# A fused three-layer block on one Trainium2 core: the state space layer's gate, skip and norm move from tokens by features to features by tokens, and the norm's root scales the output block

## The chip, the core and the metric

One core of a Trainium2 chip runs the whole program. The metric is the device time of one execution in microseconds, from the first to the last instruction with the start and the end around them; lower is better. The engines are TensorE (PE, matmuls, with its weight loads PEld), VectorE (DVE), ScalarE (ACT), GpSimd (POOL) and SyncE (SP), which here only issues transfers.

## The reference

The block takes x of 256 tokens by 2048 features through three layers: a Mamba2 state space layer, a sliding window attention layer, and a neighbourhood attention layer with an MLP. Only the first is touched. Its essence:

```python
z, xbc, dt = split(x @ w_in)                 # z: 4096 columns, 8 groups of 512
xs, B, C   = split(silu(conv4(xbc)))         # 64 heads of 64, 8 groups
y = ssd_chunked(xs, dt, a, B, C) + xs * d_skip[head]
y = y * silu(z)
yg = y.reshape(tokens, 8, 512)
yg = yg * rsqrt(mean(yg**2, over the 512) + 1e-5)
h = (yg.reshape(tokens, 4096) * norm_w) @ w_out
x = layernorm(ALPHA * x + h)
```

In ssd_chunked the part that a head adds to its outputs carries, per head and token, a factor exp(cumulated dt*a) (called the row factor below).

## The kernel before

**Products.** Every weight tile is 128 x 2048 fp32 and is split into a high part (whi, written by ACT) and a low part (wlo, written by DVE), and a product is the sum of three: high by high, low by high, high by low. The program is a list of units, one weight tile each. A unit of form "A" gives 128 features by 256 tokens: 16 matmuls of 512 columns (L1066, both parts of the activations side by side) and 16 of 256 columns with the low weights (L1070). A unit of form "B" gives 256 tokens by 512 features of a partial product, in two blocks t of 12 matmuls of 512 columns (L1087, L1089, L1091). An A unit reads its low weights only in its second half, a B unit in its third matmul.

**Rings.** whi, wlo and the raw tiles have three places each. The split of unit u+2 is written while unit u runs and may begin when unit u-1 has left the place; the transfer of unit u+5 is issued by SP when the split of u+2 has read its place. The order of the work on every engine is one hand-written script: in unit u each engine does, in this order, the emptying of unit u-1 (`late`), the split of u+2 (`hi` on ACT, `lo` on DVE), what is left of u-1 (`post`), the unit itself on PE, and the steps that a timetable puts after it. All engines run their own queue in order and meet at semaphores.

**The state space layer.** For each of the 8 groups g there are 14 units: B, C, four x units (A form; their emptying has a convolution over tokens on DVE, L1893 to L1769), four z units (B form, tokens by features, emptied by ACT's silu into zs), and the four output units ao of the group before (B form, summed into the residual XR on DVE, L1951). Four z units of group 0 stand first. Beside them runs a state space computation per group in numbered steps n = 0..13 (0..15 in groups 0 and 1, where most steps are 2 later, `late = 2`). In the units of group g the step n of group g follows unit start+n. Step by step: dif_heads (ACT L1499, L1501) writes decays for 8 heads; px turns x to tokens by features (PE L1152); xd multiplies by dt (DVE L2036) and xdk by the skip (L2045); e0, e1 are exponentials (ACT L1525), m0, m1 masks (DVE L2053); heads_out (PE L1181, L1183) gives o0 and o1, features by tokens; ACT copies them out (yT, L1529), PE turns them to tokens by features (turn_out, L1194, 8 transposes), DVE applies row factor, skip, gate and the sum of squares (L2061 to L2070), POOL takes the root (L2495), DVE scales by it (yt, L2076), PE turns y back (8 transposes, L1167), and ACT and DVE write its high part A2h (L1519) and low part A2l (L1769), which the ao units read.

**Places in PSUM.** Banks 0 to 3 go round among the units; banks 4 to 7 ("side" 0 to 3) hold the small products. A use of a side bank waits until the use before it has been emptied; the table EMPTIES names the step that empties each use.

In the notes below u17 to u20 are the units z(1,0) to z(1,3) of group 1, and u21 is ao(0,0), the first output unit.

## Time and profile before

| | |
|---|---|
| median of three runs | 2109.36 us (2108.74 to 2109.99) |
| the profiled execution: its time | 2108.5 us |
| its span, first to last instruction | 2106.5 us |
| granted TensorE clock | 1.000 |
| PE busy | 2099.5 us, 100% of the span |
| DVE busy | 1545.3 us, 73% |
| ACT busy | 1113.8 us, 53% |
| POOL busy | 52.3 us, 2% |
| DMA | 407.01 MB, mean 193 GB/s |

The state space layer's units take about the first 690 us. A matmul's record lasts longer than the time to the next one, since they overlap in the array: what a matmul costs is read from start to start. Busy shares of DVE and ACT are means over three layers; what counts is whether a split or a side product is ready when PE comes to it.

### The profile page before, as it was taken

Reading aid. Unit: us, or ns where it says so; the run is one execution under the profiler, and the core shown is the slowest. Engines: PE = TensorE matmul, PEld = TensorE weight load, DVE = VectorE, ACT = ScalarE, POOL = GpSimd, SP = SyncE. Lnnn points to the kernel's source line nnn. Section 1 sums busy time; section 2 is a strip of 40 time slices with the busy share of each in tenths; the row PEclk is TensorE's granted clock in tenths of the full one; section 3 lists DMA queues with packets and bytes.
Section 4 is the critical chain, followed back from the end, with each engine's and each line's share of the span. In section 5 each row is a group of like instructions: output and inputs, shape, how many; then the busy total and the mean of one; then the engine's idle time right before and its main releaser. Section 6 shows DMA issues by size and latency. Waiting matters only on the chain.

```text
span 2106.5 us, 27150 instructions
## 1 busy us (share of the span) xinstructions
PE 2099.5 (100%) x10752; PEld 1765.4 (84%) x10752; DVE 1545.3 (73%) x2068; ACT 1113.8 (53%) x1366; POOL 52.3 (2%) x42
## 2 busy tenths in 40 slices
PE   9999999999999999999999999999999999999999
PEld 7888888888888888888888888888888888888887
DVE  7888878768778877675675556556778688787775
ACT  6765565564554556563555445545545455455452
POOL 0000000000000000000010011000000000000000
PEclk9999999999999999999999999999999999999999
DMA  8555555555554644345564544455575666566663
GB/s 314 200 213 188 187 194 180 199 194 180 187 183 177 211 170 164 140 153 196 180 225 172 196 177 166 167 181 204 194 240 188 219 212 201 222 187 212 240 178 141
DMA packets 63710, 407.01 MB, mean 193 GB/s; under 512 B 7200, under 2 KB 9952, under 8 KB 16224
## 3 DMA queue, kind: packets, MB, share of 16 engines
q1 hardware_dynamic: 61568, 390.60, 51.5%
q0 software_dynamic: 2016, 14.68, 3.9%
q8 instruction: 85, 1.39, 0.3%
q14 instruction: 41, 0.34, 0.0%
HBM read 403.09 MB, written 2.16 MB: 192 GB/s over the span
## 4 chain that ended last, share of the span: by engine, by line
PE 99%; DVE 1%; DMA 0%; SPq 0%; POOL 0%; issue 0%; ACT 0%; DVEq 0%
PE bank L1066 22%; PE bank L1087 18%; PE bank L1091 17%; PE bank L1089 17%; PE bank L1070 11%; PE bank L1105 2%; PE bank L1103 2%; PE bank L1107 2%; PE bank L1181 1%; PE bank L1329 1%; PE bank L1265 1%; PE bank L1287 0%; PE bank L1224 0%; PE bank L1317 0%; PE bank L1194 0%; DMA raw<-wst 0%
## 5 line engine op out<-in xcount | busy, mean ns | idle before, releaser
L1809 DVE TENSOR_TENSOR wlo<-raw,whi 128x2048 fp32r<-128x2048 f32 x318 | 727.5, 2288 | 258.9 <-ACT whi L1393 226.5
L1393 ACT ACTIVATE whi<-raw 128x2048 fp32r<-128x2048 f32 x318 | 608.3, 1913 | 289.3 <-PE bank L1091 274.8
L1066 PE MATMUL bank<-A,whi 128*128 128x512 f32 x2000 | 479.2, 392 | 0.0
L1066 PEld LDWEIGHTS bank<-A,whi 128*128 128x128 f32 x2000 | 369.0, 188 | 74.3 <-issue 1.2
L1087 PE MATMUL bank<-whi,A 128*128 128x512 f32 x832 | 330.7, 397 | 0.7 <-ACT whi L1383 0.7
L1091 PE MATMUL bank<-wlo,A 128*128 128x512 f32 x832 | 325.1, 391 | 0.1
L1089 PE MATMUL bank<-whi,A 128*128 128x512 f32 x832 | 324.4, 390 | 0.0
L1087 PE MATMUL bank<-whi,A2h 128*128 128x512 f32 x800 | 314.1, 393 | 0.0
L1091 PE MATMUL bank<-wlo,A2h 128*128 128x512 f32 x800 | 311.6, 390 | 0.0
L1089 PE MATMUL bank<-whi,A2l 128*128 128x512 f32 x800 | 311.5, 389 | 0.0
L1070 PEld LDWEIGHTS bank<-A,wlo 128*128 128x128 f32 x2000 | 256.4, 191 | 9.7
L1070 PE MATMUL bank<-A,wlo 128*128 128x256 f32 x2000 | 259.4, 283 | 0.0
L1091 PEld LDWEIGHTS bank<-wlo,A 128*128 128x128 f32 x832 | 156.2, 188 | 35.7 <-DVE wlo L1797 3.1
L1087 PEld LDWEIGHTS bank<-whi,A 128*128 128x128 f32 x832 | 156.3, 188 | 34.4 <-issue 2.7
L1089 PEld LDWEIGHTS bank<-whi,A 128*128 128x128 f32 x832 | 156.4, 188 | 31.1 <-DVE A L2201 0.7
L1091 PEld LDWEIGHTS bank<-wlo,A2h 128*128 128x128 f32 x800 | 150.2, 188 | 31.6
L1087 PEld LDWEIGHTS bank<-whi,A2h 128*128 128x128 f32 x800 | 150.2, 188 | 30.6 <-issue 0.3
L1089 PEld LDWEIGHTS bank<-whi,A2l 128*128 128x128 f32 x800 | 150.3, 188 | 30.4
L1809 DVE TENSOR_TENSOR wlo<-W,whi 128x2048 fp32r<-128x2048 f32 x56 | 128.2, 2290 | 45.0 <-ACT whi L1393 44.1
L1393 ACT ACTIVATE whi<-W 128x2048 fp32r<-128x2048 f32 x56 | 107.4, 1921 | 69.3 <-DVE W L1820 46.3
L1428 ACT ACTIVATE W<-bank 128x256 f32<-128x256 f32 x60 | 23.0, 384 | 179.9 <-PE bank L1070 179.9
L2495 POOL TENSOR_TENSOR SM<-SM 128x2 f32<-128x2 f32 (+2 forms) x24 | 39.7, 1657 | 1393.5 <-DVE SM L2070 644.9
(259 smaller groups left out, 1874.7 us busy)
## 6 DMA issues: line engine op xcount, KB each, us to landing
raw<-wst SPq DMA_DIRECT2D x313, 1024.0 KB, 4.8
W<-wst SPq DMA_DIRECT2D x33, 1024.0 KB, 5.0
W<-wst POOLq DMA_DIRECT2D x9, 1024.0 KB, 8.2
W<-cum_scratch SPq DMA_DIRECT2D x8, 1024.0 KB, 7.0
W<-rows SPq DMA_DIRECT2D x21, 256.0 KB, 5.6
raw<-wst POOLq DMA_DIRECT2D x5, 1024.0 KB, 8.1
raw<-wst SPq DMA_DIRECT2D x16, 256.0 KB, 7.4
W<-nabias SPq DMA_DIRECT2D x16, 160.0 KB, 4.1
```

Of the source, the lines that this page charges most:

```text
L1066: e.matmul(o[:, :], whi[:, s, k * P:(k + 1) * P], A1[:, k, :, :].rearrange("p h t -> p (h t)"), start=k == 0, stop=False)
L1070: last = e.matmul(o[:, T:2 * T], wlo[:, s, k * P:(k + 1) * P], A1h[:, k, :], start=False, stop=k == KT - 1)
L1087: e.matmul(o, h, wh, start=opens and k == 0, stop=False)
L1089: e.matmul(o, low, wh, start=False, stop=False)
L1091: last = e.matmul(o, h, wl, start=False, stop=t in shut(tag) and k == 3)
L1103: e.matmul(o, h, wh, start=name in ("a", "b", "d", "f") and k == 0, stop=False)
L1105: e.matmul(o, low, wh, start=False, stop=False)
L1107: last = e.matmul(o, h, wl, start=False, stop=k == 3)
L1393: e.activation(whi[:, u % 3, :], raw_of(u), ACT.Copy).then_inc(*hi.inc((u, 3)))
L1428: e.activation(W[:, M_R + i % 4 * T:M_R + (i % 4 + 1) * T], rest, ACT.Copy).then_inc(*rest_a.inc(u))
L1809: e.tensor_tensor(wlo[:, u % 3, :], raw_of(u), whi[:, u % 3, :], ALU.subtract).then_inc(*lo.inc((u, 3)))
L2495: return e.tensor_tensor(SM[:, to:to + n], SM[:, src:src + n], SM[:, S_MH:S_MH + n], ALU.pow)
```

## The change

The gate, the skip, the row factor and the sum of squares now work on features by tokens, the layout in which heads_out writes.

- z of groups 1 to 7 is computed by A units (`zf`, features by tokens): 28 B units become A units. ACT copies the second half of each out, DVE adds the first, and after the fourth ACT does one silu over 1024 columns. z of group 0 stays as it was, is copied out plain, and 8 new transposes on PE (step 1) turn it; ACT's silu follows them.
- The row factor comes from DRAM: it is stored once to exp_scratch, and for every group SP loads two halves of 64 partitions (exp_load, step 8, 9 in group 1), 256 KB each as they land.
- ACT forms skip times x (`k0` to `k3`, step 8). DVE multiplies o0 and o1 by the row factor (y1), adds the skip (y2), multiplies by the gate (y3), each of the last two in one instruction of 1024 columns. ACT squares y3 (`sq`) and writes A2h from it directly, DVE writes A2l from it. The yT copies, turn_out, the back transposes, xdk and yt are gone.
- The sum of squares over 512 features: two additions on DVE (a0, a1), then two matmuls of one column on PE (`rs`, step 12 + late) into side bank 3, a small DVE step (ms, step 13 + late) and POOL's root. The root multiplies the output block as it is emptied from PSUM (`mul_add(x, ps, r, x)` in the ao units). So the A2 tiles hold y without the root.
- The residual's factor ALPHA is applied ahead, by two ACT instructions over 2048 columns in group 0, step 4.
- The transposes of the row factor (2 of the 6 in L1133) are gone.

The diff, cut to its core:

```diff
-            u += b(("z", g), "a_w_in", g * 512)
+            u += [("A", ("zf", g, i), "a_w_in", g * 512 + i * P) for i in range(4)]
...
-        if g == 0:
-            run(("ssd", 0), start, 12)
-            mid[at["z", 1, 0]].append(("ssd", 0, 12))
-            run(("ssd", 0), at["z", 1, 0], 16, 13)
-        elif g == 1:
-            run(("ssd", 1), start, 16)
-        elif g < NG - 1:
-            run(("ssd", g), start, 14)
-        else:
-            run(("ssd", g), start, 10)
-            mid[start + 10].append(("ssd", g, 10))
-            run(("ssd", g), start + 10, 14, 11)
+        run(("ssd", g), start, 16 if g < 2 else 14)
...
-            "dts": lambda: dt_v("copy"), "cb": lambda g: ssd_v("kcb", g), "px": lambda g, t: ssd_v(f"xdk{t}", g),
-            "o": lambda g, hh: ssd_a(f"yT{hh}", g), "to": lambda g, t: ssd_v(f"y1_{t}", g),
-            "yq": lambda g, pr: ssd_v(f"tl{2 * pr + 1}", g),
+            "dts": lambda: dt_v("copy"), "cb": lambda g: ssd_v("kcb", g), "px": lambda g, t: ssd_v(f"xd{t}", g),
+            "o": lambda g, hh: ssd_v(f"y1_{hh}", g), "rs": lambda g: ssd_v("ms", g), "zq": lambda i: ssd_a(f"zs{i}", 0),
...
+                if n == 12 + late:
+                    yield ("rs", g), 3
...
+            def exp_load(g):
+
+
+                w.wait_ge(s_exst, 16)
+                if g:
+                    w.wait_ge(*ssd_p("rs", g - 1))
+                src = ex_scratch.rearrange("(g f i) t -> g i f t", f=4, i=2)
+                for i in range(2):
+                    to = W[64 * i:64 * (i + 1), W_EX:W_EX + 1024].rearrange("p (f t) -> p f t", f=4)
+                    e.dma_start(to, src[g, i:i + 1].partition_broadcast(64)).then_inc(s_ex, 16)
+
             def ssd(g, n):
                 late = 2 if g < 2 else 0
+                if n == (9 if g == 1 else 8):
+                    exp_load(g)
...
+                if g == 0 and n == 1:
+                    w.wait_ge(s_ko, 16)
+                    for i in range(2):
+                        o = free(("zq", i))
+                        for t in range(NT):
+                            w.wait_ge(*evac_a((at["z", 0, 3], t)))
+                            for f in range(2):
+                                tr = e.transpose(o[:, f * T + t * P:f * T + (t + 1) * P],
+                                                 z0[t][:, (2 * i + f) * P:(2 * i + f + 1) * P], ident)
+                        tr.then_inc(*ssd_p.inc(f"z{i}", 0))
...
+                if n == 12 + late:
+                    o = free(("rs", g))
+                    w.wait_ge(*ssd_v("a1", g))
+                    for t in range(NT):
+                        mean = e.matmul(o[:, t:t + 1], ex[:, t * P:(t + 1) * P], tri[:, P:P + 1], start=True, stop=True)
+                    mean.then_inc(*ssd_p.inc("rs", g))
...
+                elif kind == "zf":
+                    w.wait_ge(*ssd_v("y3", tag[1] - 1))
+                    e.activation(zs[:, tag[2], :], rest, ACT.Copy).then_inc(*rest_a.inc(u))
...
+                elif tag[0] == "zf" and tag[2] == 3:
+                    w.wait_ge(*evac_v((u, 0)))
+                    e.activation(zs, zs, ACT.Silu).then_inc(*zs_a.inc("s", tag[1]))
...
+                if g == 0 and n == 4:
+                    for t in range(NT):
+                        w.wait_ge(s_xr[t], 16)
+                        e.activation(XR[:, t, :], XR[:, t, :], ACT.Identity, scale=ALPHA).then_inc(*xr_a.inc(str(t)))
+                if n in (7 + late // 2, 8 + late // 2):
+                    decays(g, n - 7 - late // 2)
+                if n == 8:
+                    w.wait_ge(s_co, 16)
+                    if g:
+                        w.wait_ge(*ssd_a("th3", g - 1))
+                        w.wait_ge(*ssd_v("tl3", g - 1))
+                    else:
+                        w.wait_ge(*ssd_p("z1", 0))
+                    for f in range(4):
+                        c = C_DSK + 4 * g + f
+                        w.wait_ge(*conv_a("silu", 6 * g + 2 + f))
+                        e.activation(yf[:, f, :], xf[2 + f], ACT.Identity,
+                                     scale=CO[:, c:c + 1]).then_inc(*ssd_a.inc(f"k{f}", g))
+                if n == 10 + late:
+                    w.wait_ge(*ssd_v("y3", g))
+                    e.activation(ex, y, ACT.Square).then_inc(*ssd_a.inc("sq", g))
+                    if g >= 2:
+                        w.wait_ge(*mm((at["ao", g - 2, ND - 1], 1)))
+                    for f in range(4):
+                        e.activation(A2h[:, 4 * (g % 2) + f, :], yf[:, f, :], ACT.Identity,
+                                     scale=norm_w(g, f)).then_inc(*ssd_a.inc(f"th{f}", g))
...
-                    x = xr(t, tag[2])
-                    if j == 0:
-                        w.wait_ge(*residual_ready(t, tag[2], "ao"))
-                        mul_add(x, x, ALPHA, ps, ALU.mult, ALU.add).then_inc(*evac_v.inc((u, t)))
-                    else:
-                        w.wait_ge(*evac_v((at["ao", j - 1, tag[2]], t)))
-                        e.tensor_tensor(x, ps, x, ALU.add).then_inc(*evac_v.inc((u, t)))
+                    x, r = xr(t, tag[2]), S_T + 4 + j % 2 * 2 + t
+                    w.wait_ge(*(evac_v((at["ao", j - 1, tag[2]], t)) if j else residual_ready(t, tag[2], "ao")))
+                    w.wait_ge(*ssd_g("r", j))
+                    mul_add(x, ps, SM[:, r:r + 1], x, ALU.mult, ALU.add).then_inc(*evac_v.inc((u, t)))
...
+                if n in (9 + late, 10 + late):
+                    hh = n - 9 - late
+                    half = ex[:, hh * 512:(hh + 1) * 512]
+                    w.wait_ge(*ssd_p(f"o{hh}", g))
+                    w.wait_ge(s_ex, 32 * (g + 1))
+                    e.tensor_tensor(half, side[SIDE["o", g, hh][0]][:, :], half, ALU.mult).then_inc(*ssd_v.inc(f"y1_{hh}", g))
+                if n == 10 + late:
+                    w.wait_ge(*ssd_v("y1_1", g))
+                    w.wait_ge(*ssd_a("k3", g))
+                    e.tensor_tensor(y, ex, y, ALU.add).then_inc(*ssd_v.inc("y2", g))
+                    w.wait_ge(*ssd_v("y2", g))
+                    w.wait_ge(*(zs_a("s", g) if g else ssd_a("zs1", 0)))
+                    e.tensor_tensor(yf, yf, zs, ALU.mult).then_inc(*ssd_v.inc("y3", g))
                 if n == 11 + late:
-                    w.wait_ge(*ssd_p("to", g))
-                    if g:
-                        w.wait_ge(*ssd_p("q1", g - 1))
-                    for t in range(NT):
-                        c = W_DTS + 128 + 64 * t + g * HG
-                        e.tensor_tensor(by_head(y[t]), by_head(side[SIDE["to", g, t][0]][:, :]),
-                                        per_head(W[:, c:c + HG]), ALU.mult).then_inc(*ssd_v.inc(f"y1_{t}", g))
-                        w.wait_ge(*ssd_v(f"y1_{t}", g))
-                        e.tensor_tensor(y[t], y[t], W[:, W_XD + t * 512:W_XD + (t + 1) * 512],
-                                        ALU.add).then_inc(*ssd_v.inc(f"y2_{t}", g))
-                        w.wait_ge(*ssd_v(f"y2_{t}", g))
-                        w.wait_ge(*evac_a((at["z", g, 3], t)))
-                        e.tensor_tensor(y[t], y[t], zs[:, t, :], ALU.mult).then_inc(*ssd_v.inc(f"y3_{t}", g))
-                        w.wait_ge(*ssd_v(f"y3_{t}", g))
-                        e.tensor_tensor_reduce(out=zs[:, t, :], in0=y[t], in1=y[t], scale=1.0 / 512, scalar=EPS,
-                                               op0=ALU.mult, op1=ALU.add,
-                                               accum_out=SM[:, S_T + 4 + t:S_T + 5 + t]).then_inc(*ssd_v.inc(f"ss{t}", g))
-                if n == 12 + late:
-                    w.wait_ge(*ssd_g("r", g))
-                    for t in range(NT):
-                        e.tensor_scalar(y[t], y[t], SM[:, S_T + 6 + t:S_T + 7 + t], None,
-                                        ALU.mult).then_inc(*ssd_v.inc(f"yt{t}", g))
+                    w.wait_ge(*ssd_a("sq", g))
+                    e.tensor_tensor(ex[:, 0:512], ex[:, 0:512], ex[:, 512:1024], ALU.add).then_inc(*ssd_v.inc("a0", g))
+                    w.wait_ge(*ssd_v("a0", g))
+                    e.tensor_tensor(ex[:, 0:T], ex[:, 0:T], ex[:, T:2 * T], ALU.add).then_inc(*ssd_v.inc("a1", g))
+                    if g >= 2:
+                        w.wait_ge(*mm((at["ao", g - 2, ND - 1], 1)))
+                    for f in range(4):
+                        kt = 4 * (g % 2) + f
+                        w.wait_ge(*ssd_a(f"th{f}", g))
+                        mul_add(A2l[:, kt, :], yf[:, f, :], norm_w(g, f), A2h[:, kt, :], ALU.mult,
+                                ALU.subtract).then_inc(*ssd_v.inc(f"tl{f}", g))
                 if n == 13 + late:
-                    for pr in range(2):
-                        ps = side[SIDE["yq", g, pr][0]]
-                        w.wait_ge(*ssd_p(f"q{pr}", g))
-                        if g >= 2:
-                            w.wait_ge(*mm((at["ao", g - 2, ND - 1], 1)))
-                        w.wait_ge(*ssd_a(f"th{2 * pr + 1}", g))
-                        for i in range(2):
-                            f = 2 * pr + i
-                            kt = 4 * (g % 2) + f
-                            mul_add(A2l[:, kt, :], ps[:, i * T:(i + 1) * T], norm_w(g, f), A2h[:, kt, :],
-                                    ALU.mult, ALU.subtract).then_inc(*ssd_v.inc(f"tl{f}", g))
+                    w.wait_ge(*ssd_p("rs", g))
+                    e.tensor_scalar(SM[:, S_T + 2:S_T + 4], side[SIDE["rs", g][0]][:, 0:2], 1.0 / 512, EPS, ALU.mult,
+                                    ALU.add).then_inc(*ssd_v.inc("ms", g))
...
-                if n == 11 + (2 if g < 2 else 0):
-                    w.wait_ge(*ssd_v("ss1", g))
-                    rsqrt(S_T + 6, S_T + 4, 2).then_inc(*ssd_g.inc("r", g))
+                if n == 13 + (2 if g < 2 else 0):
+                    w.wait_ge(*ssd_v("ms", g))
+                    if g >= 2:
+                        w.wait_ge(*evac_v((at["ao", g - 2, ND - 1], 1)))
+                    rsqrt(S_T + 4 + g % 2 * 2, S_T + 2, 2).then_inc(*ssd_g.inc("r", g))
```

How this moves instructions, at the places that the prediction speaks of.

ACT, around u17 and u18 in group 0's steps 12: before, from the silu of the last x unit of group 1 to the split of u20 (whi is written by L1393; L1499 and L1501 are the decays of group 1's first three heads):

```order
L1442 ACTIVATE W<-W 128x256 [waits conv_v]
L1499 ACTIVATE W<-W 128x256 [waits ssd_p0,cum_in]
L1501 ACTIVATE W<-W 128x128
L1499 ACTIVATE W<-W 128x256
L1501 ACTIVATE W<-W 128x128
L1499 ACTIVATE W<-W 128x256
L1501 ACTIVATE W<-W 128x128
L1393 ACTIVATE whi<-raw 128x2048 [waits mm_done,raw_in2]
```

Now (whi is written by L1399, the decays are L1512 and L1514, L1542 is sq, L1546 writes A2h, L1437 copies the second half of zf out):

```order
L1453 ACTIVATE W<-W 128x256 [waits conv_v]
L1542 ACTIVATE W<-W 128x1024 [waits ssd_v0]
L1546 ACTIVATE A2h<-W,CO 128x256 x4
L1512 ACTIVATE W<-W 128x256 [waits ssd_p0,cum_in]
L1514 ACTIVATE W<-W 128x128
L1512 ACTIVATE W<-W 128x256
L1514 ACTIVATE W<-W 128x128
L1512 ACTIVATE W<-W 128x256
L1514 ACTIVATE W<-W 128x128
L1437 ACTIVATE W<-bank 128x256 [waits mm_done]
L1399 ACTIVATE whi<-raw 128x2048 [waits raw_in2]
```

sq, which waits for DVE's y3, and the four A2h writes now stand ahead of the decays and of the split of u20.

DVE, the same units: before, from cb's copy of group 1 (L2027) through the splits of u20 and u21 (L1809), with the scaling by the root (L2076) and xd of group 1 (L2036) between:

```order
L2027 TENSOR_TENSOR W<-bank,KO 128x384 [waits ssd_p1]
L1809 TENSOR_TENSOR wlo<-raw,whi 128x2048 [waits mm_done,hi_done,raw_in2]
L2076 TENSOR_SCALAR W<-W,SM 128x512 [waits ssd_rms]
L2076 TENSOR_SCALAR W<-W,SM 128x512
L2036 TENSOR_TENSOR W<-bank,W 128x512 [waits ssd_p1]
L2036 TENSOR_TENSOR W<-bank,W 128x512
L1809 TENSOR_TENSOR wlo<-raw,whi 128x2048 [waits mm_done,hi_done,raw_in0]
```

Now, from the split of u19 (L1831): y1 of o1 (L2073), y2, y3, cb's copy (L2049), the emptying of the first zf unit (L1899), the split of u20, then a0, a1, A2l and xd of group 1 (L2058):

```order
L1831 TENSOR_TENSOR wlo<-raw,whi 128x2048 [waits hi_done,raw_in1]
L2073 TENSOR_TENSOR W<-bank,W 128x512 [waits ssd_p0]
L2077 TENSOR_TENSOR W<-W 128x1024 [waits ssd_v0]
L2080 TENSOR_TENSOR W<-W 128x1024 [waits ssd_v0]
L2049 TENSOR_TENSOR W<-bank,KO 128x384 [waits ssd_p1]
L1899 TENSOR_TENSOR W<-bank,W 128x256 [waits second_half_out,mm_done]
L1831 TENSOR_TENSOR wlo<-raw,whi 128x2048 [waits hi_done,raw_in2]
L2083 TENSOR_TENSOR W<-W 128x512 [waits ssd_a0]
L2085 TENSOR_TENSOR W<-W 128x256 [waits ssd_v0]
L1791 SCALAR_TENSOR_TENSOR A2l<-W,CO,A2h 128x256 [waits ssd_a0] x4
L2058 TENSOR_TENSOR W<-bank,W 128x512 [waits ssd_p1]
L2058 TENSOR_TENSOR W<-bank,W 128x512
```

a0, a1, A2l and xd of group 1 all stand behind the split of u20 in DVE's queue.

PE: the end of px of group 1 (L1176), the unit u19 (zf(1,2)), the new rs pair of group 0 (L1184, waits for both ssd_v semaphores) and the start of u20. Before, this place had no product of group 0; the back transposes (L1167) stood inside u19:

```order
L1176 MATMUL bank<-KO,W 128x128 [waits conv_a] x3
L1176 MATMUL bank<-KO,W 128x128 x4
L1080 MATMUL bank<-A,whi 128x512 [waits hi_done,emptied_v]
L1080 MATMUL bank<-A,whi 128x512 x15
L1084 MATMUL bank<-A,wlo 128x256 [waits lo_done]
L1084 MATMUL bank<-A,wlo 128x256 x15
L1184 MATMUL bank<-KO,W 128x1 [waits ssd_v0,ssd_v1]
L1184 MATMUL bank<-KO,W 128x1
L1080 MATMUL bank<-A,whi 128x512 [waits hi_done,emptied_v]
```

rs writes side bank 3, whose last use before it is px of group 1 (second block), emptied by xd of group 1 on DVE; hence the wait on two semaphores, one for a1 of group 0 and one for xd of group 1. PE does not begin u20 before rs has gone.

## Rows read from the trace of the kernel before

**Rows 1.** The page: the span, and the chain that ended last by engine.
```profile
span 2106.5 us, 27150 instructions
...
PE 99%; DVE 1%; DMA 0%; SPq 0%; POOL 0%; issue 0%; ACT 0%; DVEq 0%
```

**Rows 2.** Timeline of PE, group 6's x units: start us, duration us, then the instruction.
```profile
500.65 3.82 PE L1066 MATMUL bank<-A,whi 128*128 128x512 f32 x16
...
506.22 3.82 PE L1066 MATMUL bank<-A,whi 128*128 128x512 f32 x16
```

**Rows 3.** Timeline of PE, group 2's ao units and the transposes beside them.
```profile
304.20 0.66 PE L1194 MATMUL bank<-KO,W 128*128 128x128 f32 x4
304.61 0.48 PE L1087 MATMUL bank<-whi,A2h 128*128 128x512 f32 x1
304.93 0.39 PE L1089 MATMUL bank<-whi,A2l 128*128 128x512 f32 x1
...
309.94 0.40 PE L1091 MATMUL bank<-wlo,A2h 128*128 128x512 f32 x1
...
310.53 0.48 PE L1087 MATMUL bank<-whi,A2h 128*128 128x512 f32 x1
...
316.11 0.39 PE L1087 MATMUL bank<-whi,A2h 128*128 128x512 f32 x1
...
321.55 0.39 PE L1087 MATMUL bank<-whi,A2h 128*128 128x512 f32 x1
...
326.76 0.40 PE L1091 MATMUL bank<-wlo,A2h 128*128 128x512 f32 x1
...
327.79 2.53 PE L1066 MATMUL bank<-A,whi 128*128 128x512 f32 x10
```

**Rows 4.** Timeline of ACT in group 0; in brackets the idle time before, and its releaser.
```profile
35.36 1.28 ACT L1483 ACT_TABLE_LOAD   x1
...
67.53 0.37 ACT L1435 ACTIVATE W<-bank 128x256 f32<-128x256 f32 x1
67.79 1.90 ACT L1393 ACTIVATE whi<-raw 128x2048 fp32r<-128x2048 f32 x1
...
97.43 0.42 ACT L1442 ACTIVATE W<-W 128x256 f32<-128x256 f32 x1 [0.79 <-DVE W L1769]
```

**Rows 5.** Timeline of DVE in group 0.
```profile
37.20 0.29 DVE L1980 TENSOR_SCALAR W<-W 64x256 f32<-64x256 f32 x1 [0.88 <-ACT W L1485]
...
40.97 2.29 DVE L1809 TENSOR_TENSOR wlo<-raw,whi 128x2048 fp32r<-128x2048 f32 x1 [0.48 <-ACT whi L1393]
...
68.89 0.42 DVE L1893 TENSOR_TENSOR W<-bank,W 128x256 f32<-128x256 f32 x1
```

**Rows 6.** Timeline of DVE from the split of u19 on.
```profile
115.16 2.29 DVE L1809 TENSOR_TENSOR wlo<-raw,whi 128x2048 fp32r<-128x2048 f32 x1
117.36 0.68 DVE L2061 TENSOR_TENSOR W<-bank,W 128x512 f32<-128x512 f32 x1
...
126.40 1.28 DVE L2036 TENSOR_TENSOR W<-bank,W 128x512 f32<-128x512 f32 x2
...
129.79 1.65 DVE L1769 SCALAR_TENSOR_TENSOR A2l<-bank,CO,A2h 128x256 fp32r<-128x256 f32 x4
```

**Rows 7.** Timeline of ACT in the same stretch.
```profile
116.59 0.51 ACT L1499 ACTIVATE W<-W 128x256 f32<-128x256 f32 x1 [0.90 <-DMA W<-cum_scratch]
...
118.69 1.91 ACT L1393 ACTIVATE whi<-raw 128x2048 fp32r<-128x2048 f32 x1
...
128.07 1.57 ACT L1519 ACTIVATE A2h<-bank,CO 128x256 fp32r<-128x256 f32 x4 [3.60 <-PE bank L1167]
```

**Rows 8.** ACT groups by line and shape: busy us, mean ns, then idle before.
```profile
L1446 ACT ACTIVATE W<-W 128x1024 f32<-128x1024 f32 x4 | 4.2, 1062 | 1.2 <-DVE W L1877 1.1
```

**Rows 9.** Timeline of PE: the start of u20.
```profile
128.23 0.48 PE L1087 MATMUL bank<-whi,A 128*128 128x512 f32 x1
```

**Rows 10.** The page's DMA issues: count, KB each, median us to landing.
```profile
W<-rows SPq DMA_DIRECT2D x21, 256.0 KB, 5.6
```

129 lines of the change are left out of this document (48 added, 81 removed).

## The prediction, made before the changed kernel ran

> **What bounds the kernel now.** I read the page's chain first: PE holds 99% of it over a span of 2106.5 us [rows 1]. Then PE's timeline, start to start, because records of matmuls overlap. The reader is to see that a unit is a metronome: an A unit takes 506.22 - 500.65 = 5.57 us [rows 2], a B unit 321.55 - 316.11 = 5.44 us [rows 3], and behind a unit the side products of the state space layer cost what stands between its last matmul and the next unit's first. Nothing waits; so a change pays by the PE time it removes, and loses by every wait that it brings. DVE and ACT only have to keep their dates with PE. The stretch where they are nearest to missing them is group 0 into group 1, 60 to 130 us: there DVE goes straight from split to emptying to split [rows 6], so I followed that one.
>
> **What PE saves.** Three pieces go per group.
> - turn_out(0), four transposes behind o1: from 304.20 to 304.61, 0.41 us [rows 3].
> - turn_out(1), four alone: 309.94 to 310.53 is 0.59, less one matmul (0.23), plus 0.09 because the first matmul after a side block takes 0.32 and not 0.23 (304.61 to 304.93): 0.45 us [rows 3].
> - The eight back transposes: 326.76 to 327.79 is 1.03, less 0.23, plus 0.09: 0.89 us [rows 3].
>
> Together 1.75 us by 8 groups = 14.0; the two small transposes of the row factor give 0.1 more. 14.1 us.
>
> **What PE gets.** Eight transposes of z in group 0: 0.9, as the back transposes. 28 units go from B to A: 28 x (5.57 - 5.44) = 3.6 us; both forms stream the same number of columns, the A form in 32 matmuls and not 24. The rs pair has no row, since nothing in this trace streams one column. Above, it is two transposes of 128 x 128 in a block, 2 x 0.11 = 0.22 (0.45 / 4 and 0.89 / 8 agree on 0.11); below, nearly nothing beyond the restart of 0.09. I take the upper end, 0.24, because its stationary operand is the same 128 x 128 fp32 block: 8 x 0.24 = 1.9, with 0.7 as the low end. Sum 6.4; PE's own work falls by 7.7 us.
>
> The transposes here go by at 0.11 us each [rows 3]. The Trainium skill (TensorE: Matmul & The Clock Gate, Back-to-back issue gap) puts a matmul of 1 to 64 columns at about 60 cycles, 25 ns. By that the eight pairs would be an estimated 0.4 us instead of 1.9 and the whole sum 1.5 us lower; the same page's LDWEIGHTS rule, columns over 1.2, speaks for about 0.107 us each and for my end.
>
> **What is hidden.** The row factor's transfers, the ao emptying with a factor (a mul_add in place of an add of the same 512 columns), ms and POOL's root lie beside PE's matmuls: the root of a group is first wanted a group later, except in group 7, where it has one unit. DVE loses xdk, yt, a pass of squares and half of its small starts, ACT loses yT and gains k and sq. Neither is full on the average.
>
> **Where a wait comes in.** rs of group 0 stands in PE's queue behind u19, and everything later stands behind rs. It waits for a1 of group 0 and, because side bank 3 was last px of group 1, for xd of group 1. On DVE both stand behind the split of u20, which waits for ACT's hi of u20, and that stands behind sq and the A2h writes, which wait for y3 on DVE. So this is one chain, and I date it from the trace:
> - The earlier stretch starts 1.3 us early: z of group 0 is copied without silu, so three table loads of 1.28 us [rows 4] between 33 and 39 us go, and with them DVE's idle 0.88 and 0.48 [rows 5].
> - The scaling of the residual is two ACT instructions of 2048 columns, 1.9 each like the split [rows 4]. They stand ahead of the copy that starts at 67.53; it ends then at 67.53 + 3.7 + 0.37 = 71.6, and DVE, which began its emptying at 68.89 [rows 5], begins 2.7 later. DVE has no idle time before 117 us that doesn't itself wait for ACT, so nothing takes this up.
> - The four k copies (0.42 each with overlap, 1.4 us) meet 0.8 us of ACT idle [rows 4]: 0.6 more.
> - y1 of o0 now stands ahead of the split of u19: 0.7 more [rows 6].
>
> The split of u19 begins therefore at 115.16 - 1.3 + 2.7 + 0.6 + 0.7 = 117.9 instead of 115.16 [rows 6]. From there: the split 2.2 (117.36 - 115.16), y1 0.7, y2 and y3 1.25 each (1024 columns, between 0.68 for 512 and 2.29 for 2048 [rows 6]): y3 is done at 123.3. ACT: sq 1.06 [rows 8], A2h 1.5, three heads of decays 2.1 (118.69 - 116.59), copy 0.3, hi of u20 1.9 [rows 7]: 130.1. DVE: split 2.2, a0 0.7, a1 0.4, A2l 1.6, xd 1.3 [rows 6]: 136.3, with the semaphore 136.4.
>
> PE comes to rs at 128.23 [rows 9] - 0.45 - 0.41 - 0.89 (the pieces of group 0 that are gone) + 0.9 - 0.1 + 3 x 0.13, less 0.2 by which the first turn_out(1) was longer: 127.5. It waits 136.4 - 127.5 = 8.9 us. Afterwards both splits are ahead again (lo of u21 would end at about 139, wanted at 142.5), so the wait isn't repeated, and isn't given back either, since PE has no slack to recover.
>
> **Groups 2 to 7.** With S the start of ao(g-1,0): the running split ends at about S + 3.1, ao emptying 0.7, y1, y2, y3 3.2 make S + 6.9; sq and A2h 2.6, hi 1.9, lo 2.2 make S + 13.6; ao emptying, a0, a1 make S + 15.4. rs stands behind three B units, S + 16.3 [rows 3]. Slack 0.9: no wait, but narrow.
>
> **Sum.** Against the profiled execution, 2108.5 us: - 14.1 + 6.4 + 8.9 = + 1.2, so 2109.7. The median of the runs is 0.9 above that execution: 2110.5 us. The gain is real and one wait eats it.
>
> **The rivals.**
> - *The wait in group 0 is short.* If DVE or ACT reach y3 early enough, rs waits under 3.5 us, and below 2105.1 it counts as faster; with no wait at all 2110.5 - 8.9 = 2101.6. For it: the back part of the chain is fixed, 13.0 us after y3, but y3's date rests on four shifts. Against it: even without the residual's 2.7, 6.2 us are left, and xd alone puts rs behind one whole split. Chance 0.14.
> - *The steady groups are late too* (slower). The same chain has 0.9 us to spare in each of six groups. From 0.9 us more on it costs PE six times the excess: at 1.6 us more 6 x 0.7 = 4.2, 2114.7. Places are y1 waiting for the row factor, the A2h writes, or a1 behind a second emptying. For it: three hops between DVE and ACT, which I count without latency; against: groups 2 to 7 start from splits that are more than 6 us early. Chance 0.2.
> - *The two halves of the row factor land one after the other.* A transfer of 256 KB from rows takes 5.6 us [rows 10]; two in sequence 11.2. Issued about S - 10.3 they land at S + 0.9, DVE's y1 pushes the running split by 1.2, a1 comes at S + 16.6, and rs waits 0.3 in six groups: + 1.8, 2112.3. The Trainium skill (DMA: Bandwidth & Descriptors, Rules for kernel authors) says so: two transfers to disjoint partition halves serialize on the same engines. Chance 0.08.
> - *Forecast*, the rest: 0.58.
>
> **How the numbers follow.** The forecast's own bounds: rs pairs - 1.2, the wait 8.9 + 2 - 3, so 2106.3 to 2112.5. The range for 8 in 10 reaches into the first two rivals: 2106.0 to 2115.5. Faster or slower by over 0.2% (4.2 us, about what a measurement of this kernel can tell from no change) means under 2105.1 or over 2113.6: faster 0.14, within 0.2% 0.66, slower 0.2.
>
> **What would show it.** Idle time of PE in front of the first rs pair, 6 to 11 us, released by DVE's xd, and none in front of the other seven; transposes fewer by 122 (128 and 2 go, 8 come); A unit pitch 5.57; sq of group 0 at about 123. It is wrong if rs pairs of the steady groups show idle time, if u20 starts on its date, or if a split is late anywhere else (ao(0,0), ao(1,0)).

## The result, and the profile after

| | before | after |
|---|---|---|
| median, 6 runs each on one chip | 2109.59 us (2108.74 to 2109.99) | 2116.76 us (2116.24 to 2118.11) |
| the profiled execution | 2108.5 us | 2116.24 us |
| its span, and granted clock | 2106.5 us, 1.000 | 2114.5 us, 0.998 |
| PE, DVE, ACT busy | 2099.5, 1545.3, 1113.8 us | 2099.0, 1537.8, 1133.1 us |

The ratio is 1.0035, 95% interval 1.0022 to 1.0048: the change makes the kernel slower by 0.35%, 7.2 us by the medians. The forecast was 2110.5, range 2106.0 to 2115.5, so the time lies above the range, and on the side that had a chance of 0.2.

The chain that ended last, from the page after, against [rows 1]. PE's share fell from 99% to 91%. The profile follows the chain back to 80 us only, which takes about 4 of these points. What DVE, ACT and "issue" gained are two stretches in which it runs outside PE: from 80 to 137 us, up to PE's wait at rs of group 0, and from 300 to 332 us, up to its wait at rs of group 2.
```profile
PE 91%; DVE 2%; ACT 1%; issue 1%; DMA 0%; POOL 0%; SPq 0%; DVEq 0%
```
The waits of PE after: who waited for whom, us in total, times, longest. Two are long, at rs of group 0 (L1184, for xd) and one that the prediction has not, at px of group 1 (L1176, for kcb, DVE's copy of cb out of its bank, L2049). One is short, at rs of group 2 (L2085 is a1). The other six rs have none in this execution. The other two are as before: L1209 lies in the later, untouched layers, L1057 is the warm-up at the kernel's start.
```profile
PE bank L1184 <- DVE W L2058: 4.3, 1, 4.3
PE bank L1176 <- DVE W L2049: 3.3, 1, 3.3
PE bank L1209 <- DVE XR L2190: 1.6, 4, 0.6
PE bank L1057 <- DVE SM L1795: 1.3, 1, 1.3
...
PE bank L1184 <- DVE W L2085: 0.7, 1, 0.7
```
PE's timeline there. L1176 is px of group 1, the two L1080 rows are the first halves of u19 and u20, L1184 is rs of group 0, L1101 at 145.47 is u21. Read the durations of the first halves: 5.19 and 5.83 us, where a unit's 16 matmuls otherwise take 3.82 [rows 2].
```profile
124.42 1.52 PE L1176 MATMUL bank<-KO,W 128*128 128x128 f32 x8 [3.30 <-DVE W L2049]
125.59 5.19 PE L1080 MATMUL bank<-A,whi 128*128 128x512 f32 x16
130.62 2.07 PE L1084 MATMUL bank<-A,wlo 128*128 128x256 f32 x16
137.03 1.02 PE L1184 MATMUL bank<-KO,W 128*128 128x1 f32 x4 [4.34 <-DVE W L2058]
137.90 5.83 PE L1080 MATMUL bank<-A,whi 128*128 128x512 f32 x16
...
145.47 0.40 PE L1101 MATMUL bank<-whi,A2h 128*128 128x512 f32 x1
```
Why they take longer stands in the windows of the same trace (stretch, its length, busy time of five engines, PEclk, DMA share, GB/s). The granted clock is 1.00 up to 120 us (2.4 GHz), and behind each of the two idle stretches it is near 0.5 (1.2 GHz) for some time. Before the change it was 1.00 throughout.
```profile
126.00:129.00 3.00, 3.00 (x9) 2.33 (x9) 0.00 (x0) 3.00 (x10) 0.00 (x0) 0.61 0.00 0
...
137.50:142.50 5.00, 5.00 (x15) 4.04 (x16) 4.00 (x3) 4.99 (x8) 0.00 (x0) 0.55 0.23 74
```
The Trainium skill (TensorE: Matmul & The Clock Gate, Why this matters for your kernels) warns of this, idle gaps between bursts of matmuls that take the clock back to half; the trace agrees, 0.61 and 0.55. The prediction did not use the rule.

DVE's timeline after, the chain that the prediction dated: the split of u19, y1, y3, kcb (L2049), the split of u20, a1 (L2085), A2l, xd (L2058).
```profile
118.50 2.29 DVE L1831 TENSOR_TENSOR wlo<-raw,whi 128x2048 fp32r<-128x2048 f32 x1
120.70 0.68 DVE L2073 TENSOR_TENSOR W<-bank,W 128x512 f32<-128x512 f32 x1
...
122.68 1.23 DVE L2080 TENSOR_TENSOR W<-W 128x1024 f32<-128x1024 f32 x1
123.82 0.55 DVE L2049 TENSOR_TENSOR W<-bank,KO 128x384 f32<-128x384 f32 x1
...
130.83 2.29 DVE L1831 TENSOR_TENSOR wlo<-raw,whi 128x2048 fp32r<-128x2048 f32 x1 [1.38 <-ACT whi L1399]
...
133.76 0.42 DVE L2085 TENSOR_TENSOR W<-W 128x256 f32<-128x256 f32 x1
...
135.69 1.28 DVE L2058 TENSOR_TENSOR W<-bank,W 128x512 f32<-128x512 f32 x2
```
And ACT's: sq, A2h, three heads of decays (six rows), the copy, then hi of u20.
```profile
123.94 1.06 ACT L1542 ACTIVATE W<-W 128x1024 f32<-128x1024 f32 x1 [4.90 <-DVE W L2080]
124.90 1.69 ACT L1546 ACTIVATE A2h<-W,CO 128x256 fp32r<-128x256 f32 x4
126.50 0.49 ACT L1512 ACTIVATE W<-W 128x256 f32<-128x256 f32 x1
...
128.83 1.90 ACT L1399 ACTIVATE whi<-raw 128x2048 fp32r<-128x2048 f32 x1
```

**Where the time went.** Starts of units, after minus before, in the two profiled executions: u18 -0.2, u19 +3.7, u20 +9.7, u21 +11.7, the end of group 0's ao units +10.8. Then each steady group gives back: group 5's B unit starts 9.0 late, group 6's 8.1, group 7's 7.3, the attention layer's first unit 6.4. Up to the MLP it is still 6.6, and in the MLP, whose code is untouched, it grows to 8.0. Three questions follow: the waits and the clock behind them, the price of the rs pair, and the MLP stage.

### The profile page after: what moved, and what is told of

Same layout as the page of the kernel before. It is cut to its first block, busy times and chain, and to the rows that moved or that the text cites. A ratio compares the mean times of both kernels' runs of the same rounds, so it can differ in the third digit from the quotient of the medians.

```text
span 2114.5 us, 27498 instructions
## 1 busy us (share of the span) xinstructions
PE 2099.0 (99%) x10886; PEld 1773.8 (84%) x10886; DVE 1537.8 (73%) x2040; ACT 1133.1 (54%) x1411; POOL 53.6 (3%) x42
## 4 chain that ended last, share of the span: by engine, by line
PE 91%; DVE 2%; ACT 1%; issue 1%; DMA 0%; POOL 0%; SPq 0%; DVEq 0%
PE bank L1080 23%; PE bank L1101 15%; PE bank L1105 14%; PE bank L1103 14%; PE bank L1084 12%; PE bank L1117 2%; PE bank L1119 2%; PE bank L1121 2%; PE bank L1335 1%; DVE wlo L1831 1%; PE bank L1271 1%; PE bank L1197 1%; PE bank L1293 0%; PE bank L1230 0%; PE bank L1323 0%
## 5 line engine op out<-in xcount | busy, mean ns | idle before, releaser
L1831 DVE TENSOR_TENSOR wlo<-raw,whi 128x2048 fp32r<-128x2048 f32 x318 | 727.8, 2289 | 259.0 <-ACT whi L1399 228.7
L1399 ACT ACTIVATE whi<-raw 128x2048 fp32r<-128x2048 f32 x318 | 607.1, 1911 | 262.1 <-PE bank L1105 246.7
L1080 PE MATMUL bank<-A,whi 128*128 128x512 f32 x2448 | 590.7, 394 | 0.0
L1080 PEld LDWEIGHTS bank<-A,whi 128*128 128x128 f32 x2448 | 454.0, 189 | 93.1 <-issue 2.4
L1084 PEld LDWEIGHTS bank<-A,wlo 128*128 128x128 f32 x2448 | 313.9, 191 | 11.9
L1084 PE MATMUL bank<-A,wlo 128*128 128x256 f32 x2448 | 317.4, 283 | 0.0
L1101 PE MATMUL bank<-whi,A2h 128*128 128x512 f32 x800 | 314.2, 393 | 0.0
L1101 PE MATMUL bank<-whi,A 128*128 128x512 f32 x608 | 241.9, 398 | 0.8 <-ACT whi L1389 0.8
L1105 PE MATMUL bank<-wlo,A 128*128 128x512 f32 x608 | 237.7, 391 | 0.1
L1103 PE MATMUL bank<-whi,A 128*128 128x512 f32 x608 | 237.1, 390 | 0.0
L1101 PEld LDWEIGHTS bank<-whi,A2h 128*128 128x128 f32 x800 | 150.2, 188 | 32.1 <-issue 1.4
L1831 DVE TENSOR_TENSOR wlo<-W,whi 128x2048 fp32r<-128x2048 f32 x56 | 128.3, 2291 | 45.4 <-ACT whi L1399 44.6
L1399 ACT ACTIVATE whi<-W 128x2048 fp32r<-128x2048 f32 x56 | 107.0, 1914 | 68.9 <-DVE W L1842 45.7
L1105 PEld LDWEIGHTS bank<-wlo,A 128*128 128x128 f32 x608 | 114.1, 188 | 26.6 <-DVE wlo L1819 2.7
L1101 PEld LDWEIGHTS bank<-whi,A 128*128 128x128 f32 x608 | 114.3, 188 | 25.5 <-issue 1.7
L1103 PEld LDWEIGHTS bank<-whi,A 128*128 128x128 f32 x608 | 114.3, 188 | 23.1 <-DVE A L2208 0.7
L1791 DVE SCALAR_TENSOR_TENSOR XR<-bank,SM,XR 128x512 f32<-128x512 f32 x110 | 80.8, 746 | 16.4 <-PE bank L1105 16.3
```

The costliest lines, as they stand in the source:

```text
L1080: e.matmul(o[:, :], whi[:, s, k * P:(k + 1) * P], A1[:, k, :, :].rearrange("p h t -> p (h t)"), start=k == 0, stop=False)
L1084: last = e.matmul(o[:, T:2 * T], wlo[:, s, k * P:(k + 1) * P], A1h[:, k, :], start=False, stop=k == KT - 1)
L1101: e.matmul(o, h, wh, start=opens and k == 0, stop=False)
L1103: e.matmul(o, low, wh, start=False, stop=False)
L1105: last = e.matmul(o, h, wl, start=False, stop=t in shut(tag) and k == 3)
L1399: e.activation(whi[:, u % 3, :], raw_of(u), ACT.Copy).then_inc(*hi.inc((u, 3)))
```

## The experiments

Twelve kernels ran. Those named e1 to e4, e5 with e7 to e9, and e6 with e10 to e12 shared a chip and the runs of the kernel before, whose median was 2109.25, 2109.19 and 2109.19. Differences below are to the changed kernel's 2116.76, which was not run again beside them; the kernel before moved by 0.4 between these occasions. Steps under about 1 us are read from starts in the traces, not from medians, and as distances within one execution: the second unit of the kernel starts up to 1.2 us earlier in one execution than in another with the same code up to there.

**e1_scale_late.** ACT scales the residual later.
```diff
-                if g == 0 and n == 4:
-                    for t in range(NT):
+                if g == 0 and n in (11, 12):
+                    for t in (n - 11,):
```


> The changed kernel with one edit: ScalarE scales the residual (two instructions of 2048 columns) at steps 11 and 12 of group 0 and no longer at step 4. Theory A (one chain between VectorE and ScalarE dates both waits of TensorE, and the scaling stands in it with 2.7 us): the split behind u19, kcb of group 1 and xd all come 2.7 us earlier, u20 starts at about 135.2 and not at 137.9, time 2114.1, 2.7 below the changed kernel. Rival B (ScalarE's idle time takes the scaling up, and the waits have another source): u20 stays at 137.9 and the time at 2116.8.

Measured: 2114.53 (9 runs), -2.2. By the traces DVE's split of u19 begins at 115.41 and u20 at 134.82, both 3.1 earlier; this execution is 0.65 ahead already at its third unit, long before the edit's place, so the edit is worth 2.4, near the 2.7 of the expectation. Theory A. PE's waits in the same view:
```profile
PE bank L1184 <- DVE W L2058: 5.9, 1, 5.9
...
PE bank L1176 <- DVE W L2049: 0.9, 1, 0.9
```
The wait before px shrank by 2.4, the wait at rs grew by 1.6. Both hang on the one chain, and the second ends when xd ends, whatever the first was.

**e2_rs_later.** rs of group 0 one unit later (the same condition in the table of side banks).
```diff
-                if n == 12 + late:
+                if n == (15 if g == 0 else 12 + late):
                     o = free(("rs", g))
```


> The changed kernel with one edit: the two matmuls of the group's mean square (rs) of group 0 stand one unit later in TensorE's queue, behind u20. Theory A (rs waits for a1, and all that stands behind it waits too): no idle time in front of rs, u20 starts at about 131.5 instead of 137.9; rs then wants a1 at about 137 and finds it made; about 5.5 to 6.5 us come back, 2110.8. The wait for kcb in front of px of group 1 (3.3 us idle) stays. Rival B (a1 is not the reason; the splits themselves are late, and u21 or u22 waits for them instead): the wait only moves on, under 1.5 us come back.

Measured: 2110.53 (10 runs), -6.2. PE's timeline: no idle time at rs, which now follows u20 (the second L1080 row).
```profile
124.37 1.97 PE L1176 MATMUL bank<-KO,W 128*128 128x128 f32 x8 [3.59 <-DVE W L2049]
125.99 4.56 PE L1080 MATMUL bank<-A,whi 128*128 128x512 f32 x16
...
132.30 3.82 PE L1080 MATMUL bank<-A,whi 128*128 128x512 f32 x16
...
137.86 0.50 PE L1184 MATMUL bank<-KO,W 128*128 128x1 f32 x4
```
Theory A. Now that nothing swallows it, the wait before px costs its full 3.6 us and the slow clock behind it: from px to the low half of u19 it takes 6.0 us here and 4.5 in e5_together, which has no such wait.

**e3_cb_side0.** cb of group 1 on side bank 0.
```diff
-                    yield ("cb", g), 2
+                    yield ("cb", g), 0 if g == 1 else 2
```


> The changed kernel with one edit: cb of group 1 goes to side bank 0 as in the kernel before, not to bank 2, so that px of group 1 need not wait until VectorE has emptied it. Theory A (the end of the second wait is set by VectorE and ScalarE alone): the idle time before px (3.3 us) goes, u19 starts at about 121.5, and the wait at rs is longer by the same amount, 8 to 9 us; time unchanged within 1 us, 2116.8. Rival B (the two waits add up): 3 to 4 us come back, 2113.

Measured: 2117.36 (4 runs), +0.6, no gain: theory A for the total. Its path was other than expected. px no longer waits, the wait at rs is 6.3 us and not 8 to 9, and cb itself now waits for y1 of o0 in bank 0, which theory A had not:
```profile
117.41 1.22 PE L1167 MATMUL bank<-W 128*128 128x256 f32 x2 [2.12 <-DVE W L2073]
...
118.71 4.80 PE L1080 MATMUL bank<-A,whi 128*128 128x512 f32 x16
```
The window behind this idle stretch of 2.12 us shows the clock at 0.50 as well, and u18's first half took 4.80:
```profile
117.40:119.00 1.60, 1.59 (x5) 1.41 (x6) 1.49 (x4) 0.00 (x0) 0.00 (x0) 0.50 0.98 415
```

**e4_filled.** The gaps filled with matmuls that nobody reads.
```diff
+                if (g, n) in ((1, 7), (0, 14)):
+                    w.wait_ge(*ssd_v("y1_0", 0))
+                    for _ in range(7 if g else 13):
+                        e.matmul(side[0][:, 0:T], KO[:, 0:P], KO[:, 0:T], start=True, stop=True)
```


> The changed kernel with extra work in the two gaps: fp32 matmuls of 256 columns whose results nobody uses, 7 ahead of px of group 1 and 13 ahead of rs of group 0 (0.43 us each, 3.0 and 5.6 us), in place of idle time. Theory A (the granted clock falls behind an idle stretch, 0.61 in 126 to 129 and 0.55 in 137.5 to 142.5, and that costs u19 1.2 us, which the next wait absorbs, and u20 1.9 us, which nothing absorbs): the clock stays at 1.00 in both stretches, u20's matmuls take 5.57 us again, time 1.9 us lower, 2114.9. Rival B (u20 is slow for another reason, such as its operands or the rest of the chain): no difference or the time is up by what the extra matmuls overrun.

Measured: 2114.9 (9 runs), -1.9, as theory A. One of the nine took 5436.24 us, which nothing on record explains; the other eight lie between 2113.8 and 2115.7. The fillers (L1173), u19, rs and u20:
```profile
120.79 3.18 PE L1173 MATMUL bank<-KO 128*128 128x256 f32 x14
...
125.00 3.91 PE L1080 MATMUL bank<-A,whi 128*128 128x512 f32 x16
...
136.77 0.61 PE L1188 MATMUL bank<-KO,W 128*128 128x1 f32 x4 [0.34 <-DVE W L2062]
137.24 3.92 PE L1080 MATMUL bank<-A,whi 128*128 128x512 f32 x16
```
rs begins at nearly the old date, 136.77 instead of 137.03, but rs and its restart take 0.47 instead of 0.87, and u20 takes 5.67 (137.24 to 142.91) instead of 7.57 (137.90 to 145.47). More work on PE made the kernel faster, since the clock stayed at 1.00 in both stretches (126 to 129 and 137.5 to 142.5). The row says one more thing: 7 matmuls are recorded as x14.

**e6_sq_behind.** sq and A2h of group 0 behind hi of u20.
```diff
-                if n == 10 + late:
+                if n == (13 if g == 0 else 10 + late):
                     w.wait_ge(*ssd_v("y3", g))
```


> The changed kernel with one edit: sq and the A2h writes of group 0 stand one step later on ScalarE, behind hi of u20, so that hi of u20 no longer waits for y3 of VectorE. Theory A (the way to xd and so to rs leads over sq and A2h, 2.75 us, and over the wait for y3): hi of u20 ends about 3 us earlier, and with it the split of u20 on VectorE, a1 and xd come earlier by that and the wait at rs is under 2 us instead of 4.3, with less clock lost: 2113 to 2114; the wait before px (3.3 us) stays. Rival B (rs then waits for A2l or sq instead, which are now later): no more than 1 us comes back, 2115.8 or more.

Measured: 2109.23 (10 runs), -7.5, the ratio to the kernel before 1.000 (0.9991 to 1.0009). Theory A had the direction and much too small a size. ACT's timeline:
```profile
123.41 0.38 ACT L1437 ACTIVATE W<-bank 128x256 f32<-128x256 f32 x1 [2.89 <-DVE W L2080]
123.69 1.90 ACT L1399 ACTIVATE whi<-raw 128x2048 fp32r<-128x2048 f32 x1
125.50 1.04 ACT L1542 ACTIVATE W<-W 128x1024 f32<-128x1024 f32 x1
```
hi of u20 starts at 123.69 and not at 128.83, 5.1 earlier: not only sq and A2h (2.6) are gone from its path, but also three heads of decays (2.1), which had queued behind sq although what they need was there before; the rest is y3, 0.6 earlier in this execution. The expectation was wrong in one thing: hi of u20 still waits for y3, since the copy ahead of it (L1437) overwrites the gate that y3 reads and waits by itself. xd then ends at 131.8, PE comes to rs at 131.99, and neither the wait nor the slow clock behind it is left; 2.9 us before px stay.

**e8_rs_twice.** The rs pair issued twice.
```diff
-                    for t in range(NT):
+                    for t in (*range(NT), *range(NT)):
                         mean = e.matmul(o[:, t:t + 1], ...
```


> The changed kernel with the rs pair issued twice in each group, so the second pair's time is the price of one more pair without the restart of the stream. Theory A (each of the two matmuls is run as two passes of 0.11 us over its 128 x 128 fp32 operand, 0.45 us for a pair): 8 x 0.45 = 3.6 us more, 2120.4. Rival B, the price in the prediction (two passes of 0.11 in all, 0.24 with restart): 1.8 us more, 2118.6. By the Trainium skill (TensorE: Matmul & The Clock Gate, Back-to-back issue gap) a matmul of 1 to 64 columns is 25 ns, which would make 8 x 2 x 0.025 = 0.4 us more, 2117.2.

Measured: 2120.07 (4 runs), +3.3. The sharper reading is the length of a steady group, from the B unit of group 5 to that of group 6, in the changed kernel and here:
```profile
420.36 0.39 PE L1080 MATMUL bank<-A,whi 128*128 128x512 f32 x1
...
503.13 0.39 PE L1080 MATMUL bank<-A,whi 128*128 128x512 f32 x1
```
```profile
425.44 0.39 PE L1080 MATMUL bank<-A,whi 128*128 128x512 f32 x1
...
508.66 0.39 PE L1080 MATMUL bank<-A,whi 128*128 128x512 f32 x1
```
82.77 and 83.22: a pair costs 0.45 us. Theory A. By the Trainium skill (TensorE: Matmul & The Clock Gate, Back-to-back issue gap), 25 ns for so few columns, it would be an estimated 0.05; the measurement decides against it for this fp32 form.

The profiled execution is the slowest of the four, 2122.72 where the others took 2119.81 to 2120.15. In it the clock fell a third time, at group 2, behind an idle stretch of only 0.99 us and the doubled pair, and the next eight matmuls of 512 columns came every 0.43 us instead of every 0.23, 1.6 us lost:
```profile
334.13 1.05 PE L1184 MATMUL bank<-KO,W 128*128 128x1 f32 x8 [0.99 <-DVE W L2085]
...
335.00:338.50 3.50, 3.50 (x11) 2.73 (x11) 3.50 (x5) 0.14 (x1) 0.00 (x0) 0.53 0.44 187
```
The wait of 1.24 us at the same place in e2 left the clock at 1.00.

**e7_exp_early.** The row factor fetched two steps earlier in groups 2 to 7.
```diff
-                if n == (9 if g == 1 else 8):
+                if n == (9 if g == 1 else 8 if g == 0 else 6):
```


> The changed kernel with one edit: the two transfers of the row factor are issued at step 6 and not at step 8 in groups 2 to 7. Theory A (VectorE's y1 waits up to 4.4 us for the landing in the steady groups, but the splits run so far ahead that TensorE does not see it): VectorE's idle time in front of y1 goes, TensorE's waits stay but for at most the 0.8 us in group 2, time 2116.0 to 2116.8. Rival B (the late landing costs TensorE in each group, 0.15 us and more): 1.5 us or more come back, 2115.3 or less.

Measured: 2115.77 (6 runs). In the changed kernel DVE's y1 waits for the landing in six groups, 17.9 us in all; here that line is gone from DVE's waits:
```profile
DVE W L2073 <- DMA W<-exp_scratch: 17.9, 6, 4.4
```
PE's wait at rs of group 2 is gone too, and nothing else: between the B units of groups 4 and 7 both executions gain 2.52 us on before. That wait is where the late transfer reached PE. The changed kernel's chain, in the stretch that ends in it, passes through the landing:
```profile
309.35 6.47 DMA W<-exp_scratch
```
From the B unit of group 3 to that of group 4 it takes 83.73 us in the changed kernel and 82.77 here, as in every later group: the wait of 0.7 cost 0.96 with its restart, and that is the 1.0 of the medians. Theory A, a shade below its range.

**e5_together, e9_all_dates.** The edits of e1, e2, e3 and e6 in one; and e9 with that of e7 and this one besides (in the table of side banks too).
```diff
-                if n == 12 + late:
+                if n == (15 if g == 0 else 14 if g == 1 else 13 if g < 7 else 12):
```


> The changed kernel with four edits that touch groups 0 and 1 only: the scaling of the residual at steps 11 and 12, rs of group 0 one unit later, cb of group 1 on side bank 0, and sq with the A2h writes of group 0 one step later on ScalarE, behind hi of u20. Theory A (the whole loss of the changed kernel is the two waits on one chain and the clock behind them; with every date kept TensorE shows only its own work): no idle time before px of group 1 nor before rs of group 0, u25 starts within 0.5 of its date before (159.8), time 2106.0, from 2110.5 of the run with rs later less the 3.6 us wait before px, some 0.5 of clock and 0.6 of waiting for lo; about 0.15% under the kernel before. Rival B (another wait takes the place, at cb of group 1 for bank 0 or at u21 and u22 for their splits): 2108 to 2110.

> The four edits of the run before it and two more: rs of groups 2 to 6 stands one unit later (behind the last ao unit), and the row factor of groups 2 to 7 is fetched two steps earlier. Theory A (in group 2 rs waits for a1 by 0.8 to 1.2 us, in the others it just meets it; the transfers are hidden from TensorE): the wait of group 2 goes, 1 us less than the run before it, 2105.0. Rival B (the steady groups lose more than that through late row factors or late a1): 1.5 to 4 us less, 2102 to 2104.5. Rival C (a wait for rs or its root comes up elsewhere): no gain or a loss.

Measured: 2105.1 (11 runs), ratio 0.9981 (0.9972 to 0.9990), and 2103.97 (10 runs), ratio 0.9975 (0.9966 to 0.9984). PE's timeline of the first in the stretch that was at fault (px, u19, u20, rs) has no idle time and no stretched unit:
```profile
119.87 1.03 PE L1176 MATMUL bank<-KO,W 128*128 128x128 f32 x8
120.67 3.89 PE L1080 MATMUL bank<-A,whi 128*128 128x512 f32 x16
...
126.30 3.82 PE L1080 MATMUL bank<-A,whi 128*128 128x512 f32 x16
...
131.87 0.50 PE L1184 MATMUL bank<-KO,W 128*128 128x1 f32 x4
```
From the start of u18 to that of u21 it takes 18.0 us here, the rs pair included, against 30.2 in the changed kernel: the waits with their clock were 12.2 us of that stretch. Two short waits at rs are left, which theory A of e5 did not have: 0.9 at group 1, new, and 0.8 at group 2; u25 starts at 157.5, 2.3 ahead of the expected date and not within 0.5. For e5 theory A holds in direction and cause, with 0.9 us more than it expected. e9's edits take the wait of group 2 away and leave that of group 1 (0.97). Its gain on e5 is 1.1, as its theory A says, and the traces have it in one place, from the B unit of group 3 to that of group 4 (83.83 to 82.77); its time lies in rival B's range only because e5 came out below its forecast, and every group from the third on takes 82.77 or 82.87 us, so the steady groups did not lose more than that wait.

**e10_co_width, e12_before_shifted, e11_dates_width.** The tile CO lost 32 columns in the change, so that everything laid out behind it moved. These put them back in the changed kernel, add 32 to the kernel before, and put them back in e9.
```diff
-        CO = sb("CO", [P, NCOL])
+        CO = sb("CO", [P, NCOL + 32])[:, 0:NCOL]
```


> The changed kernel with the tile CO as wide as before (32 unused columns behind the 32 factors that are left), so that KO, SM, W and mixr, which are laid out behind it, stand again at the addresses of the kernel before and not 128 bytes lower. The question is the MLP stage, whose code is untouched and whose same 3175 matmuls take 630.0 us where they took 628.6. Theory A (some operands are read more slowly at the moved addresses): the 1.4 us come back, time 2115.3. Rival B (it comes from elsewhere, for instance from what the engines fetch or from the new buffer in main memory): the stage stays at 630.0 and the time at 2116.8.

> The kernel before with one edit: CO is 32 columns wider, nobody uses them, so that KO, SM, W and mixr stand 128 bytes higher. No instruction is changed. Theory A (the addresses matter): the MLP stage takes more than 628.6 us, by up to 1.4, if this shift is as bad as the one in the other direction. Rival B: 628.6 us, time 2109.2.

> All six edits of dates (as in the run called e9 here) and the width of CO as before. Theory A: 1.4 us less than that run's 2104.0, 2102.6. Rival B: 2104.0.

Measured: 2115.14 (9 runs), -1.6; 2110.72 (10 runs), +1.5 on the kernel before; 2102.64 (7 runs), -1.3 on e9. The MLP stage from its unit up(0,11) to the start of its last unit, in PE's timelines of before, after and e10:
```profile
1478.40 0.86 PE L1066 MATMUL bank<-A,whi 128*128 128x512 f32 x3
...
2097.64 0.39 PE L1087 MATMUL bank<-whi,A2h 128*128 128x512 f32 x1
```
```profile
1485.01 0.40 PE L1080 MATMUL bank<-A,whi 128*128 128x512 f32 x1
...
2105.63 0.39 PE L1101 MATMUL bank<-whi,A2h 128*128 128x512 f32 x1
```
```profile
1484.31 0.40 PE L1080 MATMUL bank<-A,whi 128*128 128x512 f32 x1
...
2103.55 0.39 PE L1101 MATMUL bank<-whi,A2h 128*128 128x512 f32 x1
```
619.24, 620.62 and 619.24 us, and 620.62 in e12 (1479.25 to 2099.87), at a granted clock of 1.00 each time. All 14 traces have one of the two: 619.24 in the three with the old addresses (before, e10, e11), 620.62 in the other eleven. Moving KO, SM, W and mixr by 128 bytes, in either direction, costs 1.38 us, and moving them back returns it. Theory A, shown by putting and removing it in both kernels. e11 is the fastest version: ratio 0.9967 (0.9956 to 0.9978), 0.33% under the kernel before.

The traces also say where. 1.14 of the 1.38 us fall on the 252 matmuls whose stationary operand is mixr, one of the moved tiles: start to start they take 57.68 us in the first case and 58.82 in the second, 229 and 233 ns each. The rest lies on the few matmuls behind each block of twelve of them.

## Why the prediction was wrong

**Right.** The reading of the metronome: matmul records went from 10752 to 10886, which is 122 transposes fewer, 28 x 8 for the A form and 8 x 4 for rs. A steady group is 0.85 us shorter (83.62 to 82.77), forecast 0.99. The dates of the chain came within 0.7 us, about as much as two executions of one kernel differ at their start: the split of u19 at 118.50 (forecast 117.9), y3 done at 123.9 (123.3), sq at 123.94 ("about 123"), hi of u20 done at 130.7 (130.1), xd done at 137.0 (136.3). The scaling of the residual, 2.7 in the sum, measured 2.4 (e1). e5, e9 and e11 show that the gain is real and the waits ate it: e11 is 6.6 us under the kernel before, and the forecast's own work of PE, 7.7 less, comes to 6.4 with the two corrections below (1.7 for rs, 0.4 the other way).

**"It waits 136.4 - 127.5 = 8.9 us."** The start of the split of u19 was 0.6 late in the sum, and the rest followed. Without waits PE comes from the start of u18 to rs in 12.1 us (e5: 114.22 to 126.30, where u20 now stands); from 115.31 that is 127.4, the forecast's 127.5. rs began at 137.03: 9.6 us. The term was mis-sized by 0.7.

**"Idle time of PE in front of the first rs pair, 6 to 11 us."** It was split over two places, 3.30 before px and 4.34 before rs. px of group 1 uses side bank 2, which cb of group 1 now had before it, so it waits for kcb, behind y1 to y3 on DVE. I dated the bank of rs and not that of px. Alone this costs nothing as far as e3 can show it (a wait of 2.1 at cb took its place), because the second wait absorbs the first; with rs out of the way it costs 3.6 and 1.5 of clock (e2 against e5, whose medians are 5.4 apart).

**The step that failed most: the wait is added at its length ("+ 8.9"), and the clock is put at nothing.** The sum gives no reason for that. Behind the wait at rs u20 took 1.9 us longer and rs 0.4, with a granted clock of 0.55; that is 2.3 us by the rows and 1.9 by e4. u19's 1.3 was swallowed by the wait at rs.

**"I take the upper end, 0.24."** The pair costs 0.45 (e8), so 3.6 us instead of 1.9: 1.7 too little. The upper end was no bound. The stationary operand is the one of a transpose, but a matmul in fp32 is recorded as two instructions where a transpose is one; the trace of before shows it at cb, whose one matmul of 256 columns (L1143) is this row:
```profile
114.94 0.59 PE L1143 MATMUL bank<-W 128*128 128x256 f32 x2
```

**"Slack 0.9: no wait, but narrow."** Right for groups 3 to 7 in this execution; group 2 waited 0.7, which cost 0.96 (e7), and in the executions of e6 and e10 group 3 waited as well (two waits, 1.1 and 1.2 in all). By the prediction's own sign, idle time at a steady group's rs, this step was wrong. The row factor was late on DVE in six groups, by up to 4.4 us. That is the place of the third rival, but PE saw it in group 2 alone (e7), and its mechanism was not there: in the landings of the changed kernel's trace both halves are complete 7.0 to 7.5 us after the first was issued, 8.5 in group 4, and not 11.2.

**Not in the sum at all:** the 128 bytes, 1.4 us in the MLP, 1.5 over the two later layers, and 1.6 by the medians (e10). Code that a change does not touch was taken as unchanged.

Together, by the spans of the profiled executions (2114.5 against 2106.5, + 8.0 where + 1.2 was forecast, 6.8 missed): wait 0.7, clock 2.3, rs pairs 1.7, group 2 1.0, addresses 1.5, which is 7.2. The steady groups save 0.07 more each than the sum with the corrected price of rs says (0.85 for 0.78), which takes 0.4 back and leaves 6.8. By the times of the two executions it is + 7.7, 0.3 less, which lies ahead of the first or behind the last instruction. No single one of these would have left the range; they all had one sign. None of the rivals had the whole mechanism: the second ended on the right side with another cause in the main.

## What to carry to other kernels

When two waits hang on one chain, removing either alone shows only the difference; date every bank and semaphore that the chain's engine serves, and look first for work that is queued behind a waiting instruction without needing it (e6: one step's move of sq gave 7.5 us). Price a wait on TensorE as its length plus what the next unit loses to the clock. When a tile's size changes, everything laid out behind it moves: compare untouched stages start to start, and keep the old width as a control.
